# One 512-column product for the high weights in the down projections of a Trainium2 block kernel

## What is computed

```python
D_MODEL = 1024; SEQ = 256; DEPTH = 4
D_FF = -(-8 * D_MODEL // (3 * 256)) * 256      # 2816

def swiglu(h, w_gu, w_down):
    g, u = jnp.split(h @ w_gu, 2, axis=-1)
    return (jax.nn.silu(g) * u) @ w_down

# first part, each layer
x = x + swiglu(rms_norm(x, norm_ffn[i]), ffn_w_gu[i], ffn_w_down[i])

# second part, first and last unit of each layer, for x and for ctx (mc for mx)
x = x + 0.5 * mx[2] * swiglu_2(modulated_norm(x, norm_g[l, 0], mx[0], mx[1]), *ffn1)
x = x + 0.5 * mx[8] * swiglu_2(modulated_norm(x, norm_g[l, 2], mx[6], mx[7]), *ffn2)
```

## Time and profile before

| | |
|---|---|
| median of 3 runs | 3873.91 us |
| runs | 3860.84, 3877.05, 3873.91 us |
| profiled execution, span from first to last instruction | 3866.5 us |
| TensorE busy (products) | 3718.8 us, 96% |
| TensorE busy (weight loads) | 3538.4 us, 92% |
| VectorE busy | 1620.5 us, 42% |
| ScalarE busy | 1881.5 us, 49% |
| GpSimd busy | 2635.9 us, 68% |
| mean granted TensorE clock | 0.987 |
| read from HBM | 171 GB/s over the span |

### The profile page before, as it was taken

One profiled execution on the slowest core, in us unless ns is written; L12 is line 12 of the kernel. 1 busy time (PEld: TensorE's weight loads), 2 busy tenths in 40 slices (PEclk: granted clock), 3 DMA queues, 4 the chain that ended last, 5 costly groups with the idle time before them and its releaser, 6 DMA issues.

```text
span 3866.5 us, 93381 instructions
## 1 busy us (share of the span) xinstructions
PE 3718.8 (96%) x36101; PEld 3538.4 (92%) x36101; DVE 1620.5 (42%) x3499; ACT 1881.5 (49%) x2746; POOL 2635.9 (68%) x1186
## 2 busy tenths in 40 slices
PE   8998998999899898899999999999999999999998
PEld 7778997998699767799999999999999999999998
DVE  6544315315642664433222474753223222276442
ACT  5325446544454431545555555465555555555643
POOL 5005873885288400388888878768888888886886
PEclk9999999999999999999999999999999999999999
DMA  6555662664366355466666646546666666664664
GB/s 187 197 194 145 190 175 80 185 194 121 84 188 191 109 184 190 122 190 190 191 191 194 192 143 190 154 144 203 193 191 191 190 185 199 188 188 130 184 180 141
DMA packets 1162954, 664.98 MB, mean 172 GB/s; under 512 B 30157, under 2 KB 1122201, under 8 KB 1162551
## 3 DMA queue, kind: packets, MB, share of 16 engines
q1 hardware_dynamic: 1162679, 661.06, 57.9%
HBM read 659.92 MB, written 1.05 MB: 171 GB/s over the span
## 4 chain that ended last, share of the span: by engine, by line
PE 57%; issue 26%; POOL 12%; DVE 3%; ACT 1%; DMA 1%; POOLq 0%; DVEq 0%; SPq 0%; ACTq 0%
PE bank L861 55%; POOL wlo L621 12%; PE bank L840 1%; DVE bank L3060 1%; DMA raw<-in_w_in 0%; PE bank L1062 0%; ACT whi L631 0%; DMA raw<-in_ffn_w_gu 0%; PE bank L961 0%; POOLq L620 0%; DVE W L1985 0%; DVE W L1998 0%; DVE W L1983 0%; POOLq L101 0%; PE bank L2701 0%
## 5 line engine op out<-in xcount | busy, mean ns | idle before, releaser
L621 POOL TENSOR_TENSOR wlo<-raw,whi 128x1024 fp32r<-128x1024 f32 (+3 forms) x1182 | 2635.7, 2247 | 1206.8 <-ACT whi L631 1200.6
L631 ACT ACTIVATE whi<-raw 128x1024 fp32r<-128x1024 f32 (+3 forms) x1182 | 1171.5, 996 | 1066.5 <-PE bank L861 905.0
L861 PE MATMUL bank<-AH,whi 128*128 128x256 f32 (+1 forms) x5712 | 1595.6, 279 | 24.2 <-DVE AL L771 9.8
L861 PE MATMUL bank<-AL,whi 128*128 128x256 f32 x5712 | 1588.1, 278 | 0.0
L861 PE MATMUL bank<-AH,wlo 128*128 128x256 f32 (+1 forms) x5712 | 1587.5, 278 | 0.0
L861 PEld LDWEIGHTS bank<-AH,whi 128*128 128x128 f32 x5712 | 1079.0, 189 | 33.5 <-issue 19.4
L861 PEld LDWEIGHTS bank<-AH,wlo 128*128 128x128 f32 x5712 | 1077.7, 189 | 0.0
L861 PEld LDWEIGHTS bank<-AL,whi 128*128 128x128 f32 x5712 | 1076.9, 189 | 0.6
L861 PE MATMUL bank<-HH,whi 128*128 128x256 f32 x1936 | 538.1, 278 | 0.0
L861 PE MATMUL bank<-HH,wlo 128*128 128x256 f32 x1936 | 536.0, 277 | 0.0
L861 PE MATMUL bank<-HL,whi 128*128 128x256 f32 x1936 | 536.0, 277 | 0.0
(11 more groups left out here) (449 smaller groups left out, 4911.7 us busy)
## 6 DMA issues: line engine op xcount, KB each, us to landing
raw<-in_ffn_w SPq DMA_DIRECT2D x420, 512.0 KB, 4.0
raw<-in_w_in SPq DMA_DIRECT2D x182, 512.0 KB, 3.9
raw<-in_ffn_w_gu SPq DMA_DIRECT2D x176, 512.0 KB, 3.8
ada_raw<-in_w_ada SPq DMA_DIRECT2D x96, 512.0 KB, 5.8
raw<-in_ffn_w_down SPq DMA_DIRECT2D x64, 512.0 KB, 3.8
raw<-in_rw_w_rkv SPq DMA_DIRECT2D x48, 512.0 KB, 3.7
raw<-in_w_ada SPq DMA_DIRECT2D x48, 512.0 KB, 5.8
raw<-in_ffn_w SPq DMA_DIRECT2D x56, 384.0 KB, 3.5
```

The costliest lines, as they stand in the source:

```text
L621: pool.tensor_tensor(wlo[slot][:, 0:n], raw[slot][:, 0:n], whi[slot][:, 0:n], ALU.subtract).then_inc(lo_ready, 1)
L631: act.activation(whi[slot][:, 0:n], raw[slot][:, 0:n], ACT.Copy).then_inc(hi_ready, 1)
L861: mm = pe.matmul(ps[:, 0:o.shape[2]], w, o[:, k0 + c, :], start=tile not in started and c == n == 0, stop=last_panel and c == nk - 1 and n ...
```

## The change

In the eleven down projections, and only there, the two products of the high weights of a chunk become one. The operand parts `HH` and `HL` are now halves of one tile, `HHL`, so that an access pattern of 2 x 256 columns reaches the same chunk of both, and the result goes to all 512 columns of the step's bank: the first half gets high weights times high operand, the second half high weights times low operand. The low weights' product adds to the first half. VectorE then adds both halves to the stream, one after the other, the second waiting for the first, and frees the bank after the second. The order of steps, panels and transfers is the same.

```diff
-def dense(name, w, col, n_out, operand, kc=C, tokens_out=False):
+def dense(name, w, col, n_out, operand, kc=C, tokens_out=False, halves=False):
@@
-        HH = sb("HH", FC * S, F32R, at=w_at[0])
-        HL = sb("HL", FC * S, F32R, at=w_at[0] + FC * S * 4)
+        HHL = sb("HHL", 2 * FC * S, F32R, at=w_at[0])
+        HH, HL = HHL[:, 0:FC * S], HHL[:, FC * S:2 * FC * S]
@@
-        HID = (v3(HH), v3(HL))
+        HID = (v3(HH), v3(HL), HHL[:, :].rearrange("p (k c t) -> p c k t", k=2, t=S))
@@
-            plan(dense(f"{name}.down", w_down, 0, D, HID, kc=FC))
+            plan(dense(f"{name}.down", w_down, 0, D, HID, kc=FC, halves=True))
@@
-                dve_tiles(dve, name, take_residual(dve, x, gate))
+                dve_tiles(dve, name, take_residual(dve, x, gate, g.halves), {dve_step: 1} if g.halves else None)
@@
                         wh, wl = (t[slot][:, c * P:(c + 1) * P] for t in (whi, wlo))
+                        if g.halves:
+                            pe.matmul(ps[:, :].rearrange("p (k t) -> p k t", k=2), wh, parts[2][:, k0 + c],
+                                      start=tile not in started and c == 0, stop=False)
+                            mm = pe.matmul(ps[:, 0:S], wl, oh[:, k0 + c, :], start=False, stop=last_panel and c == nk - 1)
+                            continue
                         for n, (w, o) in enumerate(((wh, oh), (wh, ol), (wl, oh))):
@@
-        def take_residual(dve, x, gate=None):
+        def take_residual(dve, x, gate=None, halves=False):
 
             def take(s, j, banks):
                 o = x[:, bass.ds(s * S, S)]
-                if gate is None:
+                if halves and gate is None:
+                    dve.tensor_tensor(o, o, banks[0][:, 0:S], ALU.add).then_inc(dve_step, 1)
+                    dve.wait_ge(dve_step, after(dve, dve_step))
+                    dve.tensor_tensor(o, o, banks[0][:, S:2 * S], ALU.add).then_inc(bank_free, 1)
+                elif halves:
+                    k = gate[:, bass.ds(s, 1)]
+                    dve.scalar_tensor_tensor(o, banks[0][:, 0:S], k, o, ALU.mult, ALU.add).then_inc(dve_step, 1)
+                    dve.wait_ge(dve_step, after(dve, dve_step))
+                    dve.scalar_tensor_tensor(o, banks[0][:, S:2 * S], k, o, ALU.mult, ALU.add).then_inc(bank_free, 1)
+                elif gate is None:
```

10 lines of the change are left out of this document (6 added, 4 removed).

## The result

The changed kernel is slower: 3906.18 us median of 5 runs (3898.72 to 3917.44) against 3874.29 us for the kernel before (3860.84 to 3877.05, 5 runs). The ratio on record, which is not worked out from these two medians (their quotient is 1.0082), is 1.0076, 95% interval 1.005 to 1.0102. The forecast was 3857.7 us, with a range up to 3882: the time came out on the other side and outside the range. The profiled execution of the changed kernel has a span of 3906.9 us, 40.4 us more than the profiled one of before (3866.5). That is more than the 32 us between the medians, because the profiled execution of before was one of its quicker ones.

The account below looks back on a forecast made before the run. The prediction took TensorE to bound the down projections, with GpSimd at 87% behind it. Its terms, 13.5 + 2.8 - 0.1 = 16.2 us saved, taken from the median of 3873.91 us, gave 3857.7 us, range 3845 to 3882.

Parts of the forecast that it names:

- What bounds the kernel: Down projections: TensorE and its weight loads busy all 59.9 us of one, GpSimd behind it with 52.35 us.
- The load sets the pace and the 256 columns hide behind it: Products of 256 columns: the 128-column weight load takes 109 ns of the 113.4 ns interval, streaming barely hidden behind it.
- the 8-column group: A group of 32 products streaming only 8 columns behind full 128-column loads: 109 ns each, taken as the load's time.
- 215.5 ns for the 512-column product: Merged product of each down-projection chunk: interval taken from the norm sums, which stream twice 256 columns in one record.
- 116.5 ns for the exposed load: Interval behind each chunk's 256-column product, where the next high weights' load is exposed; put between 113.4 and 118 ns.
- 1682 chunks gain 8.0 ns: Down projections: 1936 chunks less 210 and 44 held by waits, each going from 340 to 332.0 ns; 13.5 us saved.
- The late panel and f20x.down: Chunks before fixed waits gain nothing: 30 in each of seven projections before the 14th panel (210), 44 in f20x.down.
- VectorE's second addition: One more operation of 0.42 or 0.48 us in each of 88 steps, nearly all hidden; 0.1 us lost in all.
- (c): Rival, 0.12: merged downs hand the slow pace to five up stages, costing 24.3 us; kernel at 3884.5 us.
- (b): Rival, 0.12: the merged product's two operand pieces stream like two products, 227 ns; chunk stays 340 ns, kernel 3874 us.
- (d): Rival, 0.02: the merged product costs no more than a load, chunk 227 ns; GpSimd becomes the bound, kernel 3803 us.

Follow-up runs that it names:

- the ruler: Run 5: changed kernel plus groups of 48 products of several widths behind the last down projection; 117.7 ns an interval at 256 columns, 233.4 at 512.
- run 10: Kernel before with one 512-column product added at the head of the five up stages that follow a down projection; 3900.42 us, ratio 1.0037.
- run 13: Changed kernel with one 512-column product added at the head of the second panel of the five up stages; 3918.83 us, ratio 1.0096.
- run 14: Kernel before with one 512-column product added at the head of the second panel of the five up stages; 3896.82 us, one time.
- run 3: Changed kernel with the merge alone undone: three 256-column products a chunk into two half banks, second addition kept; 3888.79 us, ratio 0.9997.
- run 1: Changed kernel with a chunk's high and low parts side by side, so the 512-column operand is one piece; 3910.71 us, ratio 1.0061.
- run 2: Changed kernel without the low weights' product in the down projections, leaving the 512-column product alone; 3802.7 us, one time.
- run 7: Kernel before, unchanged, in another execution; 3881.91 us.
- run 8: Changed kernel plus groups behind the last down: alternating 512 and 256 columns, none or one of another width, then 256; 117.8 ns directly behind the alternation.

## Why the prediction was wrong, step by step

**What bounds the kernel: right.** TensorE bounds both kinds of stage, before and after, and GpSimd stays under it (52.12 of 62.07 us in ffn0.down).

**"The load sets the pace and the 256 columns hide behind it": wrong by a few ns, and this is where the error starts.** There is a floor, as the 8-column group said (109 ns in the earlier trace rows, 111 in the ruler). But the streaming of 256 columns is of the same size and just above it: by the ruler's 0.456 ns a column it is 116.7 ns, and 512 columns took twice as long as 256 at either pace (runs 10, 13 and 14). A merge saves a load only in so far as the load was not hidden behind streaming, and it was hidden. Even with both products at the fast pace, 226 + 113.3, the chunk would be 339.3 ns, level with the 340 of before: at this streaming rate the change can't win from a fast kernel.

**"215.5 ns for the 512-column product": the step that failed.** It measured 235.3 in the kernel and 232 to 233.4 in a row of its like. I had taken it from the norm sums, records of another format that go through TensorE at another rate. The nearest row was not a row of the same thing; twice the interval of the products in question, 227 to 236 ns, stood in the earlier trace rows and would have been the better guess. The chunk was put at 332.0 and measured 353.3: 19.8 ns of the error are here, 1.5 in the other term. The Trainium skill (TensorE: Matmul & The Clock Gate, Back-to-back issue gap) gives 131 ns as the sustained spacing at 512 columns. The runs don't bear it out for this format: 232 ns with every load hidden.

**"116.5 ns for the exposed load": a small miss.** It was 118, always. In the alternation the slow pace is not a draw: in the downs of every run with the merged pair, and in the ruler, a pair took some 353 ns.

**"1682 chunks gain 8.0 ns": turned round.** A chunk loses 13.3 ns against a fast one (340) and nothing against a slow one (353.3). That is 176 x 13.3 = 2.3 us for a down that had been fast, which is what ffn0 to ffn2 and f21x lost, and it is why f10x.down and f11x.down, whose second halves had been slow, lost 1.0 instead of 2.1. The sum of the terms was -16.2 us; the downs came to +19.3.

**The late panel and f20x.down.** With TensorE slower, these waits shrink instead of growing: the hosts lost 2.1 us where the others lost 2.3, so the late panel's wait gave some 0.2 us back. The judgement that these chunks don't gain was never put to the test, since none did.

**VectorE's second addition: right.** Behind ffn0.down (engines in order of time, the answer to the earlier trace rows) the squares start as the second addition ends, and TensorE's 16 sums run through:

```profile
542.09 3.62 PE L977 MATMUL bank<-W,ones 128*128 128x256 f32 x16
...
542.41 0.42 DVE L933 TENSOR_TENSOR X<-X,bank 128x256 f32 x1 [6.90 <-PE bank L865]
542.86 0.42 DVE L935 TENSOR_TENSOR X<-X,bank 128x256 f32 x1
543.25 0.71 ACT L813 ACTIVATE W<-X 128x256 f32<-128x256 f32 x2
```

3.62 us against 3.61 before, and run 3 puts the whole of it at a ratio of 0.9997. The pair starts 0.45 us apart, not 0.55.

**The rivals.** What happened is (c) with something like the price of (b). (b) put the 512-column product at 227 ns because of the two pieces; run 1 shows that the pieces are not the reason and runs 2 and 5 that the width alone is. (b)'s price itself is what 512 columns cost in a fast stretch (225 to 226 ns); at the pace that the alternation keeps it is 235. (c) had the mechanism of the other half: the merged rhythm hands the slow pace to the five up stages. It put 24.3 us on them, and they lost 23.4. I gave it 0.12 and named for it that a down "hands one of the two paces" on. I let it keep the gain of 13.7 us, so it ended at 3884.5. With the downs at +19.3 in its place the same sum gives 3874 + 24.3 + 19.3 = 3918, against 3906.18 measured. Part of that difference is likely that executions of before have slow stretches of their own (ffn0.down in run 7), and where a down is slow already the change costs it nothing. The chances treated (b) and (c) as either-or. They were separate questions (how fast does it stream, what does it hand on), and the case in which both went wrong had no place in the range.

**(d): fell**, with the 232 ns of run 2.

## What to carry to other kernels

Before merging two products to save a weight load, ask if the load is on the path at all: at 256 columns of this format the floor that fits the load (111 ns) and the streaming (113 to 118 ns) are of one size, and a product of twice the columns costs twice the interval (226 and 235 ns). Take the price of a wider product from rows of the same format, by intervals between starts, and not from another kind of product with the same number of columns. And look at the stages behind the edit too: here more than half of the loss was in stages without a changed instruction, and the chain of waits with its counts (124.37 us for 1056 products against 119.6) shows it at a glance.

## What the runs showed of the hardware

**Two paces.** Products of 256 columns of this format in a row run at 113.3 or at 117.8 ns, at a granted clock of 1.00 in both, with or without other engines at work. The pace lasts until something disturbs it, across the end of a stage too, over more than 1500 products in the earlier trace rows. The kernel before settles in one or the other behind its waits, not the same in each execution (ffn0.down 59.73 and 62.07 us in two profiles). A single product of 512 columns takes 225 to 226 ns in a fast stretch and 233 to 236 in a slow one.

**What selects.** An alternation of 512 and 256 columns runs at 353.3 ns a pair in the kernel and in the ruler, and it is followed by the slow pace (50 of 50 stages; 5 of 35 behind three products of 256). A single 512-column product in a fast stretch turned it slow 8 times of 8 in the kernel. What brings the fast pace back there is open: 8, 288 and 512 columns in the up stages of the changed kernel did not, although 272, 288 and 384 columns did so each time in run 8 (240 every other time). The traces show starts and not what goes on inside TensorE, so why there are two paces stays open as well.

**Load and streaming.** Behind full loads the interval is 111 ns, the same for 128 to 224 columns of streaming. A load of half the columns brought nothing at 256 or 512; 16 products of 128 columns with half loads came 59 ns apart in the kernel before. Streaming, in groups of one width: 133.4, 146.6, 173.4 and 233.4 ns for 288, 320, 384 and 512 columns.
